# Norm factor as a diagonal matrix in the turn of token tiles, all tiles loaded at once, two weight tiles on the first 512 tokens

## The chip, the core and the metric

One core of a Trainium2 chip. The time is device microseconds of one execution, the median of three runs. The engines are TensorE (PE, with its weight loads as PEld), VectorE (DVE), ScalarE (ACT), GpSimd (POOL) and SyncE (SP), which issues most DMAs.

## What is computed

One layer of a hybrid encoder block on 1024 tokens of 1024 features, in float32. The change touches only its first step and its first projection:

```python
hn = x * rsqrt(mean(x * x, -1) + EPS) * attn_norm     # RMSNorm
proj = hn @ w_in                                      # 1024 x 2728 columns
# proj feeds three head groups: gated delta rule, pooling, latent attention
x = x + concat(groups) @ w_out
x = x + (silu(gate) * up) @ w_down                    # SwiGLU on RMSNorm(x)
```

## The kernel before

The code is written by hand for five engines, each with its own program, which meet at counted semaphores: `wait_ge(sem, n)` holds an engine's whole program until the count is reached, and everything behind it waits too.

**Turn.** The projection needs tokens along the free axis, so the eight tiles of 128 tokens (TT = 8) are normalised and turned. Per tile t: ACT squares x and sums along the row (L1048, `x_sumsq`), running three tiles ahead; POOL makes the factor (L874, L875, `x_rstd`); VectorE scales x by it (L1320, `x_scale`, into `x_scaled`, `raw_used`); TensorE transposes the eight 128x128 blocks into a pair of PSUM banks (L1808, `x_turned`); VectorE multiplies by the gain of `attn_norm` into `stage` (L1329, `x_gain`, `bank_pair_free`); ACT rounds to the high part `act_hi` (L1061, `stage_read`); VectorE subtracts for the low part `act_lo` (L1336, `x_low`, `h_ready`). VectorE's order is scale t+1, low t-1, gain t.

**Projection.** Every product is three passes of f32r: high x high, high x low, low x high. `gemm` (L1812 to L1833) takes 8 k-blocks, 3 passes and 2 halves of 512 tokens: 48 matmuls per weight tile (L1829). Tile m = 0 is a narrow one of 40 columns (`small_raw`: the gates and the rotary key), split in two: its first half may start at `h_ready` = 4, the second at 8; both also need its `w_lo` (L1347). Tiles m = 1 to 21 have 128 columns. ACT makes `w_hi` and VectorE `w_lo` of tile m + 2 when `gemm_done` reaches m + 1 (two slots). After tile 1 stand small transposes (L1846) of what tile 0 gave.

**Loads.** Four buffers `raw` hold first x tiles, then w_in tiles. SP issues in order: x 0 to 3, small_raw, six constants, x 4 to 7 (each waiting until the scale of tile t - 4 has freed its buffer, L525), six more small loads, then w_in tiles (L554, waiting on `raw_used`), with 2 MB of zeros written after m = 2 (L605). ACT issues eight loads of small rows, which VectorE and TensorE turn into `cols` (L1801, L1802, L1314) before the first tile.

## Time and profile before

| | us |
|---|---|
| Runs before, median of 3 | 1370.69 |
| Lowest, highest | 1370.59, 1374.19 |
| The profiled execution's own time | 1367.57 |
| Its span | 1365.7 |
| TensorE busy in the span | 1278.0 (94%) |
| VectorE, ACT, POOL busy | 803.4, 458.5, 392.0 |
| Mean granted clock of TensorE | 0.969 of full |

The profile is of one execution. Times of rows are from the start of its span. The chain of waits is followed back from the last instruction, so what stands on it sets the end. A duration of a matmul is its latency; the distance from start to start is what one costs in a row of them. The granted clock is 1.00 at 2.4 GHz and 0.50 at 1.2 GHz.

### The profile page before, as it was taken

The page shows a single profiled execution, that of the slowest core. Times are in us where ns is not written, and L with a number is a line of the kernel's source. Part 1 is how long each engine was busy: PE and PEld are TensorE (multiplying, and loading weights), DVE is VectorE, ACT ScalarE, POOL GpSimd, SP SyncE. Part 2 cuts the span into 40 slices and gives each one's busy share as a digit, 9 for nine tenths or more (in the row PEclk, how much of TensorE's full clock was granted, in tenths as well). Part 3 has the DMA queues.
Part 4 walks back from the last instruction along what each step waited for, and adds up shares of the span by engine and source line. Part 5 has one row for each costly group of instructions (what it writes and reads, how often), then busy time and mean ns, then how long its engine had stood idle before and what let it go on. Part 6 is the DMA issues. An engine that isn't in the chain of part 4 may idle for free.

```text
span 1365.7 us, 17092 instructions
## 1 busy us (share of the span) xinstructions
PE 1278.0 (94%) x6028; PEld 1011.6 (74%) x6028; DVE 803.4 (59%) x1290; ACT 458.5 (34%) x758; POOL 392.0 (29%) x359
## 2 busy tenths in 40 slices
PE   4899999999788888899978899999999998999998
PEld 3588777887577777744446788888888886888886
DVE  5436788466265655522345466665565559686776
ACT  4231332441332333312234233333333344243442
POOL 3001011330122121200163575565646526200000
PEclk7899999999899999999989999999999999999999
DMA  6411243535722211012131566564456338665634
GB/s 195 127 48 31 74 121 106 151 132 131 239 75 60 75 46 58 0 65 104 47 93 47 169 218 213 187 209 160 154 188 251 127 98 291 204 212 153 212 114 164
DMA packets 188980, 182.62 MB, mean 134 GB/s; under 512 B 19486, under 2 KB 145772, under 8 KB 188908
## 3 DMA queue, kind: packets, MB, share of 16 engines
q1 hardware_dynamic: 188784, 181.64, 42.3%
q8 instruction: 43, 0.70, 0.2%
q14 instruction: 29, 0.24, 0.1%
q10 hardware_dynamic: 124, 0.04, 0.0%
HBM read 123.97 MB, written 56.62 MB: 132 GB/s over the span
## 4 chain that ended last, share of the span: by engine, by line
PE 77%; DVE 11%; issue 5%; ACT 3%; POOL 2%; DMA 1%; SPq 0%; ACTq 0%; DVEq 0%; POOLq 0%; PEldq 0%
PE ps L2161 30%; PE ps L2166 13%; PE ps L1829 12%; PE ps L2077 8%; PE ps L1953 5%; PE ps L2026 3%; PE ps L2054 2%; PE ps L2042 1%; DVE stage L1475 1%; DVE row_stat L1678 1%; POOL mla_sc L895 1%; DVE dop_lo L1734 1%; DVE x L1791 1%; PE ps L1958 1%; PE ps L1974 1%
## 5 line engine op out<-in xcount | busy, mean ns | idle before, releaser
L2161 PE MATMUL ps<-xop_hi,wop_hi 128*128 128x512 f32 x616 | 242.5, 394 | 17.6 <-DVE wop_lo L1728 10.2
L2161 PE MATMUL ps<-xop_hi,wop_lo 128*128 128x512 f32 x616 | 242.0, 393 | 0.0
L2161 PE MATMUL ps<-xop_lo,wop_hi 128*128 128x512 f32 x616 | 241.9, 393 | 0.0
L2161 PEld LDWEIGHTS ps<-xop_hi,wop_hi 128*128 128x128 f32 x616 | 117.0, 190 | 44.1 <-DVE wop_lo L1728 11.2
L2161 PEld LDWEIGHTS ps<-xop_hi,wop_lo 128*128 128x128 f32 x616 | 116.9, 190 | 24.5
L2161 PEld LDWEIGHTS ps<-xop_lo,wop_hi 128*128 128x128 f32 x616 | 116.9, 190 | 24.3
L2166 PE MATMUL ps<-dop_hi,wop_hi 128*128 128x512 f32 x308 | 121.2, 394 | 7.3 <-DVE x L1791 7.3
L1728 DVE TENSOR_TENSOR wop_lo<-w_sumS,wop_hi 128x512 fp32r<-128x512 f32 (+1 forms) x104 | 85.4, 823 | 70.4 <-ACT wop_hi L1250 70.4
L2166 PE MATMUL ps<-dop_hi,wop_lo 128*128 128x512 f32 x308 | 120.6, 392 | 0.0
L2166 PE MATMUL ps<-dop_lo,wop_hi 128*128 128x512 f32 x308 | 120.6, 392 | 0.0
L1829 PE MATMUL ps<-act_hi,w_hi 128*128 128x512 f32 (+1 forms) x352 | 116.4, 408 | 3.8 <-DVE w_lo L1347 3.6
L1728 DVE TENSOR_TENSOR wop_lo<-w_pair,wop_hi 128x512 fp32r<-128x512 f32 (+1 forms) x78 | 88.1, 1132 | 46.8 <-ACT wop_hi L1250 46.8
L2077 PE MATMUL ps<-w_out_sb,oT 128*128 128x512 f32 x256 | 111.4, 592 | 0.0
L1829 PE MATMUL ps<-act_lo,w_hi 128*128 128x512 f32 (+1 forms) x352 | 111.1, 393 | 0.0
L1829 PE MATMUL ps<-act_hi,w_lo 128*128 128x512 f32 (+1 forms) x352 | 111.0, 393 | 0.0
L1791 DVE TENSOR_TENSOR x<-x,ps 128x512 f32<-128x512 f32 x112 | 76.6, 684 | 42.2 <-PE ps L2166 42.1
L2077 PEld LDWEIGHTS ps<-w_out_sb,oT 128*128 128x128 f32 x256 | 47.9, 190 | 56.9 <-issue 56.9
L1354 DVE TENSOR_TENSOR w_lo<-raw,w_hi 128x1024 fp32r<-128x1024 f32 x21 | 26.2, 1250 | 98.1 <-ACT w_hi L1066 98.1
L1250 ACT ACTIVATE wop_hi<-w_sumS 128x512 fp32r<-128x512 f32 (+1 forms) x104 | 63.2, 609 | 60.5 <-PE ps L2161 37.0
L1829 PEld LDWEIGHTS ps<-act_hi,w_hi 128*128 128x128 f32 (+1 forms) x352 | 64.8, 187 | 22.6 <-issue 5.5
L1829 PEld LDWEIGHTS ps<-act_lo,w_hi 128*128 128x128 f32 (+1 forms) x352 | 65.6, 186 | 15.6 <-issue 0.7
L1829 PEld LDWEIGHTS ps<-act_hi,w_lo 128*128 128x128 f32 (+1 forms) x352 | 65.4, 186 | 15.8 <-issue 1.0
(281 smaller groups left out, 2156.2 us busy)
## 6 DMA issues: line engine op xcount, KB each, us to landing
w_pair<-in_w_gate_up SPq DMA_DIRECT2D x44, 512.0 KB, 5.4
hidden<-up SPq DMA_DIRECT2D x22, 512.0 KB, 3.0
wd_rows<-in_w_down SPq DMA_DIRECT2D x22, 512.0 KB, 4.9
raw<-in_w_in SPq DMA_DIRECT2D x21, 512.0 KB, 4.3
wd_raw<-down_sums SPq DMA_DIRECT2D x12, 768.0 KB, 8.5
...
```

Of the source, the lines that this page charges most:

```text
L895: pool.tensor_tensor(mla_sc[t % 2][:, 24:32], mla_sc[t % 2][:, 16:24], half_neg[:, 0:8], ALU.pow).then_inc(mla_pow, 1)
L1250: act.activation(wop_hi[q % RING][:, 0:kh, :], src, ACT.Copy).then_inc(wop_high, 1)
L1354: dve.tensor_tensor(w_lo[slot][:, :, :], raw[rawslot][:, :, :], w_hi[slot][:, :, :].bitcast(f32), ALU.subtract).then_inc(raw_used, 1)
L1728: dve.tensor_tensor(wop_lo[q % RING][:, 0:kh, :], src, wop_hi[q % RING][:, 0:kh, :].bitcast(f32), ALU.subtract).then_inc(wop_ready, 1)
L1791: dve.tensor_tensor(part, part, bank, ALU.add).then_inc(added, 1)
L1829: last = pe.matmul(ps[0:rows, pair + h, :], w[:, k, 0:rows], a[:, k, h * BANK:(h + 1) * BANK], start=(k == 0 and w is whi and a is a_hi), ...
L1953: last = pe.matmul(ps[:, out_bank, h * P:(h + 1) * P], lhs(h), rhs(h), start=True, stop=True)
L2026: last = pe.matmul(ps[:, 4 + h, 0:n], qh[0:QK, t * P:(t + 1) * P], kT[0:QK, ds(i, 1), h * BANK:h * BANK + n].rearrange("p a n -> p (a n)") ...
L2054: last = pe.matmul(ps[:, 7, 0:V_DIM], probsT[0][:, j, :], V[:, kt, ds(i, 1), :].rearrange("p a d -> p (a d)"), start=(kt == 0), stop=(kt = ...
L2077: last = pe.matmul(ps[:, op_pair[t] + h, :], oT[:, t, k, :], w_out_sb[:, k, h * BANK:(h + 1) * BANK], start=(k == 0), stop=(k == KT - 1))
L2161: last = pe.matmul(ps[:, bank, :], w[:, k, :], a[:, k, :], start=(p in ("P1", "P2", "P7") and k == 0 and w is wop_hi[s] and a is hi), stop ...
L2166: last = pe.matmul(ps[:, bank, :], w[:, k, :], a[:, k, :], start=(p in ("P1", "P2", "P7") and k == 0 and w is wop_hi[s] and a is hi), stop ...
```

## The change

- VectorE no longer scales. POOL multiplies the identity by the factors of the tile's tokens (`x_diag`, two of them), and TensorE multiplies each block of raw x with that matrix moving, so that one product turns and scales it.
- Tiles 4 to 7 go to places of their own (the three `cT` rows and one `pz` row, used later by others), so all eight loads wait for no buffer; the second four wait once for the small rows. The constants are issued after weight tile 2, the zeros after weight tile 6.
- Turning uses PSUM banks 4 to 7, so banks 0 to 3 can hold weight tiles 0 and 1 for both halves. Their first halves over tokens 0 to 511 run around the last turn (`early_gemm`), their second halves after `h_ready` = 8. The splits of `small_raw` and of weight tile 1 move into the turn.
- VectorE's order becomes gain t, low t-1; `x_gain(t)` still waits for `h_ready` of t - 1.
- `raw_used` no longer counts the eight scales, so `N_X` goes; counts that used it are renumbered.

```diff
--- before.py
+++ after.py
@@ -254,7 +254,8 @@
     kr_sq = sgT[:, 3, 576:832].rearrange("p (t n) -> p t n", t=TT)
     assert KT * SMALL <= 320
     x_sq = prep[:, 0, :]
-    x_scaled = [prep[:, 1 + s, :] for s in range(2)]
+    x_diag = [prep[:, 1 + s, 0:P] for s in range(2)]
+    x_in = [raw[t][:, :, :].rearrange("p k n -> p (k n)") for t in range(RAW)] + [cT[:, j, :] for j in range(3)] + [pz[:, 0, :]]
     C_CONV, C_ATTN, C_FFN, C_QA, C_KVA, C_GDN, C_POOL, C_POS, C_QK = 0, 48, 56, 64, 66, 67, 68, 70, 78
     ctx = ExitStack()
...
@@ -508,9 +509,11 @@
         def raw_round(gi, j):
             return (j // 3 if gi == 0 else (3, 0, 2, 2)[raw_slot(gi, j)] + ((gi - 1) * 7 + j) // 4) + 1
-        def loaded_count(n):
-            return 16 * (n // RAW + 1) - (16 if n % RAW == 0 else 0)
+        def loaded_count(m):
+            return 16 * (1 + m // RAW + (1 if m % RAW else 0))
+        def x_here(t):
+            return (x_loaded[t], 16) if t < RAW else (x_late[t - RAW], 16)
         w_in_v = w_in[0].rearrange("(k p) n -> p k n", p=P)
@@ -519,39 +522,37 @@
         @block.sync
         def _(sp):
-            def load_x(t):
-                if t >= RAW:
-                    sp.wait_ge(raw_used, t - RAW + 1)
-                sp.dma_start(raw[t % RAW][:, :, :].rearrange("p k n -> p (k n)"),
-                             x[0, t * P:(t + 1) * P, :]).then_inc(x_loaded[t % RAW], 16)
             for t in range(RAW):
-                load_x(t)
+                sp.dma_start(x_in[t], x[0, t * P:(t + 1) * P, :]).then_inc(x_here(t)[0], 16)
             sp.dma_start(small_raw[:, :, 0:2 * GDN_HEADS], w_in_v[:, :, OFF_A:OFF_POOL]).then_inc(small_loaded, 16)
             sp.dma_start(small_raw[:, :, 2 * GDN_HEADS:SMALL],
                          w_in_v[:, :, OFF_KR:OFF_KR + ROPE]).then_inc(small_loaded, 16)
-            sp.dma_start(ab_rows[:, 0, :], a_log[0].partition_broadcast(P)).then_inc(prep_loaded, 16)
-            sp.dma_start(ab_rows[:, 1, :], dt_bias[0].partition_broadcast(P)).then_inc(prep_loaded, 16)
-            sp.dma_start(wuq[:, :, :], w_uq[0].rearrange("(k p) n -> p k n", p=P)).then_inc(prep_loaded, 16)
-            sp.dma_start(wukv[:, :], w_ukv[0]).then_inc(prep_loaded, 16)
-            sp.dma_start(qk_gain[:, 0, :], q_norm[0].partition_broadcast(P)).then_inc(prep_loaded, 16)
-            sp.dma_start(qk_gain[:, 1, :], k_norm[0].partition_broadcast(P)).then_inc(prep_loaded, 16)
+            sp.wait_ge(rows_loaded, 8 * 16)
             for t in range(RAW, TT):
-                load_x(t)
-            sp.wait_ge(consts_ready, 1)
-            for g in range(POOL_GROUPS):
-                lo = (g % 2) * POOL_DIM
-                sp.dma_start(pw[lo:lo + POOL_DIM, g // 2, lo:lo + POOL_DIM], pool_w[0, g]).then_inc(pw_loaded, 16)
-            for j, gain in enumerate((q_norm, k_norm)):
-                sp.dma_start(cols[0:NOPE, C_QK + j:C_QK + j + 1],
-                             gain[0, 0:NOPE].rearrange("(p o) -> p o", o=1)).then_inc(pw_loaded, 16)
+                sp.dma_start(x_in[t], x[0, t * P:(t + 1) * P, :]).then_inc(x_here(t)[0], 16)
+            def load_constants():
+                sp.dma_start(ab_rows[:, 0, :], a_log[0].partition_broadcast(P)).then_inc(prep_loaded, 16)
+                sp.dma_start(ab_rows[:, 1, :], dt_bias[0].partition_broadcast(P)).then_inc(prep_loaded, 16)
+                sp.dma_start(wuq[:, :, :], w_uq[0].rearrange("(k p) n -> p k n", p=P)).then_inc(prep_loaded, 16)
+                sp.dma_start(wukv[:, :], w_ukv[0]).then_inc(prep_loaded, 16)
+                sp.dma_start(qk_gain[:, 0, :], q_norm[0].partition_broadcast(P)).then_inc(prep_loaded, 16)
+                sp.dma_start(qk_gain[:, 1, :], k_norm[0].partition_broadcast(P)).then_inc(prep_loaded, 16)
+                sp.wait_ge(consts_ready, 1)
+                for g in range(POOL_GROUPS):
+                    lo = (g % 2) * POOL_DIM
+                    sp.dma_start(pw[lo:lo + POOL_DIM, g // 2, lo:lo + POOL_DIM], pool_w[0, g]).then_inc(pw_loaded, 16)
+                for j, gain in enumerate((q_norm, k_norm)):
+                    sp.dma_start(cols[0:NOPE, C_QK + j:C_QK + j + 1],
+                                 gain[0, 0:NOPE].rearrange("(p o) -> p o", o=1)).then_inc(pw_loaded, 16)
             def load_in_tile(m, s):
-                sp.wait_ge(raw_used, N_X + m - RAW + 1)
+                if m <= RAW:
+                    sp.wait_ge(x_turned, m % RAW + 1)
+                else:
+                    sp.wait_ge(raw_used, m - RAW + 1)
                 sp.dma_start(raw[s][:, :, :], w_in_v[:, :, ds(proj_col(m), P)]).then_inc(x_loaded[s], 16)
             def keep_qkv(f):
@@ -588,7 +589,9 @@
             KEEP_LAG = 7
             for m in range(1, IN_ALL + KEEP_LAG):
                 if m < IN_ALL:
-                    load_in_tile(m, (N_X + m) % RAW)
+                    load_in_tile(m, m % RAW)
+                if m == 2:
+                    load_constants()
                 done = m - KEEP_LAG
                 if M_QKV <= done < M_GATE:
                     keep_qkv(done - M_QKV)
...
@@ -872,8 +875,11 @@
             for t in range(TT):
                 pool.wait_ge(x_sumsq, t + 1)
                 link(pool.tensor_scalar(meansq[:, t:t + 1], ssq[:, t:t + 1], 1.0 / D_MODEL, EPS, ALU.mult, ALU.add))
-                pool.tensor_tensor(rstd[:, t:t + 1], meansq[:, t:t + 1], half_neg[:, 0:1],
-                                   ALU.pow).then_inc(x_rstd, 1)
+                link(pool.tensor_tensor(rstd[:, t:t + 1], meansq[:, t:t + 1], half_neg[:, 0:1], ALU.pow))
+                if t >= 2:
+                    pool.wait_ge(x_turned, t - 1)
+                pool.tensor_tensor(x_diag[t % 2], ident[:, :], rstd[:, t:t + 1].broadcast_to([P, P]),
+                                   ALU.mult).then_inc(diag_ready, 1)
             pool.memset(zeros[:, :, :], 0.0).then_inc(zeros_ready, 1)
...
@@ -1042,10 +1048,10 @@
             def x_square(t):
-                act.wait_ge(x_loaded[t % RAW], 16 * (t // RAW + 1))
+                act.wait_ge(*x_here(t))
                 if t >= 1:
                     act.wait_ge(x_sumsq, t)
-                act.activation(x_sq, raw[t % RAW][:, :, :].rearrange("p k n -> p (k n)"), ACT.Square,
+                act.activation(x_sq, x_in[t], ACT.Square,
                                accum_out=ssq[:, t:t + 1]).then_inc(x_sumsq, 1)
             AHEAD = 3
@@ -1054,9 +1060,12 @@
             for t in range(TT):
                 if t + AHEAD < TT:
                     x_square(t + AHEAD)
-                if t == TT - 2:
+                if t == 2:
                     act.wait_ge(small_loaded, 2 * 16)
                     act.activation(w_hi[0][:, :, 0:SMALL], small_raw, ACT.Copy).then_inc(hi_split, 1)
+                if t == 5:
+                    act.wait_ge(x_loaded[1], loaded_count(1))
+                    act.activation(w_hi[1][:, :, :], raw[1][:, :, :], ACT.Copy).then_inc(hi_split, 1)
                 act.wait_ge(bank_pair_free, t + 1)
                 act.activation(act_hi[:, :, tile_cols(t)], stage[t % 2][:, :].rearrange("p (k n) -> p k n", k=KT),
                                ACT.Copy).then_inc(stage_read, 1)
@@ -1065,17 +1074,12 @@
                 act.wait_ge(x_loaded[rawslot], rnd)
                 act.activation(w_hi[slot][:, :, :], raw[rawslot][:, :, :], ACT.Copy).then_inc(hi_split, 1)
-            def in_round(m):
-                return loaded_count(N_X + m)
-            split_hi(1, 1, 1, in_round(1))
             act.wait_ge(sin_args, 1)
             act.activation(trig[:, :, :, :].rearrange("p a t f -> p (a t f)"), sin_in, ACT.Sin).then_inc(trig_ready, 1)
             for m in range(M_QKV):
                 act.wait_ge(gemm_done, m + 1)
-                split_hi(m + 2, m % 2, (N_X + m + 2) % RAW, in_round(m + 2))
+                split_hi(m + 2, m % 2, (m + 2) % RAW, loaded_count(m + 2))
                 if M_CQ <= m < M_POOL:
                     act.wait_ge(bank_pair_free, TT + m + 1)
                     act.activation(c_sq[:, m - 1, :], cT[:, m - 1, :], ACT.Square).then_inc(lat_squared, 1)
...
@@ -1311,21 +1315,14 @@
             dve.wait_ge(rows_loaded, 8 * 16)
             dve.tensor_copy(pos_f, pos_i[0:TT, :]).then_inc(pos_float, 1)
             dve.wait_ge(cols_in_psum, 1)
-            link(dve.tensor_copy(cols[:, 0:C_POS + TT], ps[:, 7, 0:C_POS + TT]))
-            def x_scale(t):
-                dve.wait_ge(x_rstd, t + 1)
-                if t >= 2:
-                    dve.wait_ge(x_turned, t - 1)
-                dve.tensor_scalar(x_scaled[t % 2], raw[t % RAW][:, :, :].rearrange("p k n -> p (k n)"),
-                                  rstd[:, t:t + 1], None, ALU.mult).then_inc(raw_used, 1)
+            link(dve.tensor_copy(cols[:, 0:C_POS + TT], ps[:, 3, 0:C_POS + TT]))
             def x_gain(t):
                 dve.wait_ge(x_turned, t + 1)
                 if t >= 2:
                     dve.wait_ge(h_ready, t - 1)
-                pair = (t % 2) * 2
+                pair = 4 + (t % 2) * 2
                 dve.tensor_tensor(stage[t % 2][:, :].rearrange("p (k n) -> p k n", k=KT),
                                   ps[:, pair:pair + 2, :].rearrange("p a (k n) -> p (a k) n", n=P),
                                   cols[:, C_ATTN:C_ATTN + KT].unsqueeze(2).broadcast_to([P, KT, P]),
@@ -1336,17 +1333,18 @@
                 dve.tensor_tensor(act_lo[:, :, tile_cols(t)], stage[t % 2][:, :].rearrange("p (k n) -> p k n", k=KT),
                                   act_hi[:, :, tile_cols(t)].bitcast(f32), ALU.subtract).then_inc(h_ready, 1)
-            x_scale(0)
             for t in range(TT):
-                if t + 1 < TT:
-                    x_scale(t + 1)
+                x_gain(t)
                 if t >= 1:
                     x_low(t - 1)
-                if t == TT - 1:
+                if t == 3:
                     dve.wait_ge(hi_split, 1)
                     dve.tensor_tensor(w_lo[0][:, :, 0:SMALL], small_raw, w_hi[0][:, :, 0:SMALL].bitcast(f32),
                                       ALU.subtract).then_inc(raw_used, 1)
-                x_gain(t)
+                if t == 6:
+                    dve.wait_ge(hi_split, 2)
+                    dve.tensor_tensor(w_lo[1][:, :, :], raw[1][:, :, :], w_hi[1][:, :, :].bitcast(f32),
+                                      ALU.subtract).then_inc(raw_used, 1)
             x_low(TT - 1)
             def split_lo(m, slot, rawslot):
@@ -1389,8 +1387,6 @@
             def pair_of(m):
                 return ps[:, (m % 2) * 2:(m % 2) * 2 + 2, :].rearrange("p a n -> p (a n)")
-            split_lo(1, 1, 1)
             ang_v = ang.rearrange("p (t f) -> p t f", t=TT)
             link(dve.tensor_tensor(ang_v, cols[:, C_POS:C_POS + TT].unsqueeze(2).broadcast_to([P, TT, HALF]),
                                    inv_freq.unsqueeze(1).broadcast_to([P, TT, HALF]), ALU.mult))
...
@@ -1798,26 +1794,35 @@
             pe.wait_ge(consts_ready, 1)
             pe.wait_ge(pos_float, 1)
-            pe.transpose(ps[:, 7, 0:C_POS], rows, ident[0:C_POS, 0:C_POS])
-            pe.transpose(ps[:, 7, C_POS:C_POS + TT], pos_f, ident[0:TT, 0:TT]).then_inc(cols_in_psum, 1)
-            for t in range(TT):
-                pe.wait_ge(raw_used, t + 1)
+            pe.transpose(ps[:, 3, 0:C_POS], rows, ident[0:C_POS, 0:C_POS])
+            pe.transpose(ps[:, 3, C_POS:C_POS + TT], pos_f, ident[0:TT, 0:TT]).then_inc(cols_in_psum, 1)
+            def turn_x(t):
+                pe.wait_ge(diag_ready, t + 1)
                 if t >= 2:
                     pe.wait_ge(bank_pair_free, t - 1)
                 for k in range(KT):
-                    last = pe.transpose(ps[:, (t % 2) * 2 + k // 4, (k % 4) * P:(k % 4 + 1) * P],
-                                        x_scaled[t % 2][:, k * P:(k + 1) * P], ident[:, :])
+                    last = pe.matmul(ps[:, 4 + (t % 2) * 2 + k // 4, (k % 4) * P:(k % 4 + 1) * P],
+                                     x_in[t][:, k * P:(k + 1) * P], x_diag[t % 2], start=True, stop=True)
                 last.then_inc(x_turned, 1)
-            def gemm(whi, wlo, a_hi, a_lo, pair, kts, signal, rows=P, tail=None, late_half=None, middle=None):
-                passes = [(0,), (1,)] if late_half else [(0, 1)]
-                for halves in passes:
-                    if halves == (1,):
-                        pe.wait_ge(*late_half)
+            def early_gemm(m, h, ks):
+                rows = SMALL if m == 0 else P
+                for k in ks:
+                    for w, a in ((w_hi[m], act_hi), (w_hi[m], act_lo), (w_lo[m], act_hi)):
+                        last = pe.matmul(ps[0:rows, 2 * m + h, :], w[:, k, 0:rows], a[:, k, h * BANK:(h + 1) * BANK],
+                                         start=(k == 0 and w is w_hi[m] and a is act_hi), stop=(k == KT - 1 and w is w_lo[m]),
+                                         skip_group_check=True)
+                return last
+            for t in range(TT - 1):
+                turn_x(t)
+            def gemm(whi, wlo, a_hi, a_lo, pair, kts, signal, rows=P, tail=None, middle=None):
+                for halves in [(0, 1)]:
                     for k in range(kts):
                         if tail and k == kts - 1:
                             pe.wait_ge(*tail)
@@ -1834,12 +1839,20 @@
             pe.wait_ge(h_ready, TT // 2)
-            pe.wait_ge(raw_used, N_X + 1)
-            gemm(w_hi[0], w_lo[0], act_hi, act_lo, 0, KT, gemm_done, SMALL, late_half=(h_ready, TT))
+            pe.wait_ge(raw_used, 1)
+            early_gemm(0, 0, range(0, KT // 2))
+            turn_x(TT - 1)
+            early_gemm(0, 0, range(KT // 2, KT))
+            pe.wait_ge(raw_used, 2)
+            early_gemm(1, 0, range(KT))
+            pe.wait_ge(h_ready, TT)
+            early_gemm(0, 1, range(KT)).then_inc(gemm_done, 1)
+            early_gemm(1, 1, range(KT)).then_inc(gemm_done, 1)
             for m in range(1, M_QKV):
-                pe.wait_ge(raw_used, N_X + m + 1)
-                pe.wait_ge(bank_pair_free, TT + m - 1)
-                gemm(w_hi[m % 2], w_lo[m % 2], act_hi, act_lo, (m % 2) * 2, KT, gemm_done)
+                if m >= 2:
+                    pe.wait_ge(raw_used, m + 1)
+                    pe.wait_ge(bank_pair_free, TT + m - 1)
+                    gemm(w_hi[m % 2], w_lo[m % 2], act_hi, act_lo, (m % 2) * 2, KT, gemm_done)
                 if m == 1:
                     pe.wait_ge(bank_pair_free, TT + 1)
                     for t in range(TT):
...
```

## Rows read from the trace of the kernel before

**Rows 1.** The chain of waits, 0 to 70 us: start us, us, what.

```profile
24.09 1.23 DVE stage L1329
38.66 24.18 PE ps L1829 x96
```

**Rows 2.** Timeline of one period: start, us, engine, line, op [idle before <-releaser].

```profile
25.23 0.75 DVE L1320 TENSOR_SCALAR prep<-raw,rstd 128x1024 f32<-128x1024 f32 x1
26.03 1.97 PE L1808 MATMUL ps<-ident,prep 128*128 128x128 f32 x8 [1.52 <-DVE prep L1320]
26.44 1.22 DVE L1336 TENSOR_TENSOR act_lo<-stage,act_hi 128x1024 fp32r<-128x1024 f32 x1 [0.46 <-ACT act_hi L1061]
27.58 1.22 DVE L1329 TENSOR_TENSOR stage<-ps,cols 128x1024 f32<-128x1024 f32 x1
```

**Rows 3.** TensorE's waits, 0 to 130 us: total us, times, longest.

```profile
PE ps L1808 <- DVE prep L1320: 11.0, 7, 3.0
```

**Rows 4.** Windows: us, then PE, PEld, DVE, ACT, POOL busy, PEclk, DMA, GB/s.

```profile
22.50:24.60 2.10, 1.97 (x8) 1.56 (x8) 1.65 (x2) 1.46 (x3) 0.47 (x2) 0.50 0.04 1
42.00:42.90 0.90, 0.90 (x3) 0.37 (x2) 0.90 (x1) 0.90 (x1) 0.00 (x0) 0.50 0.31 75
42.90:44.00 1.10, 1.10 (x6) 0.61 (x5) 1.00 (x5) 0.09 (x1) 0.00 (x0) 0.95 0.08 19
```

**Rows 5.** The timeline, the first turns and GpSimd's first step.

```profile
6.33 0.19 POOL L874 TENSOR_SCALAR meansq<-ssq 128x1 f32<-128x1 f32 x1 [2.18 <-ACT prep L1048]
9.50 0.27 PE L1802 MATMUL ps<-ident,prep 8*128 8x8 f32 x1
10.89 3.67 PE L1808 MATMUL ps<-ident,prep 128*128 128x128 f32 x16 [1.12 <-DVE prep L1320]
18.32 1.26 PE L1808 MATMUL ps<-ident,prep 128*128 128x128 f32 x8 [2.00 <-DVE prep L1320]
```

**Rows 6.** The timeline, two chained operations on VectorE.

```profile
45.66 0.30 DVE L1409 TENSOR_SCALAR prep<-prep 128x256 f32<-128x256 f32 x1
45.99 0.42 DVE L1410 TENSOR_TENSOR prep<-prep 128x256 f32<-128x256 f32 x1
```

**Rows 7.** Single operations: the timeline, then a group by form.

```profile
24.32 0.55 POOL L875 TENSOR_TENSOR rstd<-meansq,half_neg 128x1 f32<-128x1 f32 x1
25.35 1.06 ACT L1061 ACTIVATE act_hi<-stage 128x1024 fp32r<-128x1024 f32 x1 [1.39 <-DVE stage L1329]
26.31 1.04 ACT L1048 ACTIVATE prep<-raw 128x1024 f32<-128x1024 f32 x1
27.26 0.19 ACT L1048 ACTIVATION_READ_ACCUMULATOR prep<-raw 128x1 f32 x1
38.03 0.49 DVE L1347 TENSOR_TENSOR w_lo<-sgT,w_hi 128x320 fp32r<-128x320 f32 x1
...
L904 POOL TENSOR_TENSOR gtg<-gt,g_log 128x512 f32<-128x512 f32 x8 | 8.2, 1044 | 0.0
```

**Rows 8.** Transfers: chain (last small row), line L526 (x tiles), timeline (tile 4).

```profile
3.44 5.36 DMA pos_i<-in_positions
...
DMA to landing us min/median/max: 4.1/5.4/7.1
...
17.34 1.06 ACT L1048 ACTIVATE prep<-raw 128x1024 f32<-128x1024 f32 x1 [2.12 <-DMA raw<-in_x]
```

**Rows 9.** The timeline: clock up, weight tile 1 begins, what follows it.

```profile
42.92 0.44 PE L1829 MATMUL ps<-act_lo,w_hi 128*40 128x512 f32 x1
51.78 0.62 PE L1829 MATMUL ps<-act_hi,w_hi 128*128 128x512 f32 x2
62.76 0.58 PEld L1846 LDWEIGHTS ps<-ident,prep 40*128 40x128 f32 x8 [0.35 <-issue]
```

**Rows 10.** The chain, whole span: f32 128x128 multiplies L1953, transposes L2069.

```profile
365.52 1.84 PE ps L1953 x16
573.04 1.94 PE ps L2069 x16
```

16 lines of the change are left out of this document (8 added, 8 removed).

## Prediction, made before the changed kernel was run

> **What bounds the kernel now.** I read the page first (TensorE is busy 94% of the span), then the chain of waits over the first 70 us, the timeline of that stretch, and the granted clock by windows. The chain shows two pieces there. Up to 38.66 us it alternates between the stages of turning a token tile; from 38.66 us on it is TensorE's own projection, 96 matmuls without a wait [rows 1]. So everything that starts or shortens those 96 matmuls (weight tiles 0 and 1) moves the end, and after them nothing is tied to the clock on the wall: later stages count on `gemm_done` and `raw_used`.
>
> In the turn VectorE sets the pace. One period, from one gain multiply to the next, is 27.58 - 24.09 = 3.49 us [rows 1, 2]: scale L1320 0.75, low part L1336 1.22, gain L1329 1.22, and gaps in which VectorE waits for what it had asked of others. TensorE waits 11.0 us in seven places for the scaled tile [rows 3], and needs 1.97 us of each period for its eight transposes, since its clock is at half there [rows 2, 4].
>
> **Part by part.** Removed: eight scales on VectorE (0.75 each). Added: on GpSimd one 128x128 multiply per tile; TensorE multiplies raw x by the diagonal in place of transposing scaled x. Moved: x tiles 4 to 7 no longer wait for a buffer; six constants and the 2 MB of zeros go behind them on SP; the halves of tiles 0 and 1 over the first 512 tokens go ahead of the last turn.
>
> *Start.* Turn 0 stood behind the first scale, at 10.89 us; now the diagonal hangs on the sum of squares, which GpSimd takes up at 6.33 us [rows 5]; its three operations there, some 0.2 + 0.6 + 0.4 with gaps, end by 7.8 us. So turn 0 follows the transposes of the rows directly: 9.50 + 0.27, about 9.84 us. Sixteen took 3.67 us [rows 5], so turn 1 ends at 13.5 and the gain of tile 1 starts at 13.6.
>
> *VectorE's new period.* Gain, low, gain, low. A following independent instruction starts 1.14 us after the last (26.44 to 27.58) [rows 2], but the gain of t+1 now waits for the low part just before it, so it is 1.22 and the wait on its own completion, 0.03 us by the chained pair at 45.66 [rows 6]: 1.26. A period is 2.41. Gains start at 13.6, 16.0, 18.4; then low 2, the small w_lo (0.49 [rows 7]), and gain 4 at 21.15, ending 22.4. Low 3 ends at 23.5: four tiles ready.
>
> *What else could set that pace.* ACT needs 1.04 + 0.19 for a square and 1.06 for a high part [rows 7], 2.3 against 2.41: it just fits, and the small w_hi (a third of a tile, so under 0.5) goes into its lead. GpSimd needs 0.19 [rows 5], 0.55 and the new multiply. The trace has no 128x128 one; bounds are a quarter of L904's 1.04, 0.26, and the whole of it [rows 7]. I take 0.4. The diagonal of tile 6 is then ready at about 21.8, against 22.4 when its bank is free; at 1.04 it is 22.4, so the cost is nil, and 0.3 beyond. TensorE at half clock needs 1.97 per tile, under 2.41.
>
> *Loads.* SP waits for the rows, landed at 3.44 + 5.36 = 8.80, then issues x 4 to 7. An x tile lands 4.1 to 7.1 us after issue [rows 8], so x 4 is there between 13.0 and 16.0; ACT wants it at 14.2. In the worst case high part 1 ends at 18.3 where VectorE wants it at 17.15: 0 to 1.15 us, and I take 0, the first of a group of four landing early. In the kernel before, ACT got tile 4 only at 17.34 [rows 8], but there the transfer could not be issued before the first scale had freed its buffer, at about 10.9. The constants on SP stand in front of weight tile 3 alone, which nobody needs before the end of tile 1 (about 50 us): over 30 us of cover from their start near 16 us. The eight issues of zeros, moved to m = 6, are in front of weight tile 7, used some 40 us later. Both at nothing; without the cover each would cost what it is late.
>
> *TensorE from there.* Turn 6 runs 22.4 to 24.4, then the early halves. Until the clock rises a matmul takes (42.92 - 38.66)/10 = 0.426, after it (51.78 - 42.92)/38 = 0.233 for tile 0; tile 1's 48 take 62.76 - 51.78 = 10.98 [rows 1, 9]. In the rows the granted clock is 0.50 (the level of 1.2 GHz) until the projection has run some 4.3 us, then full (2.4 GHz) [rows 4]. So: 10 x 0.426 = 4.26, 38 x 0.233 = 8.86, 10.98, and one warm turn 1.26 [rows 5] in their midst: 25.36, ending at 49.8 us instead of 62.76. **Saving 13.0 us.** All 48 first-half matmuls end near 38.5; the eighth low part, behind the last turn, ends near 34, so the second halves don't wait (4 us of slack). The small w_lo and tile 1's, at 21.1 and 29.7, are early as well.
>
> *The multiply in place of the transpose.* Sixteen real f32 128x128 multiplies take 1.84 us and sixteen f32 transposes 1.94 [rows 10]: no difference. I take a ratio of 1. The Trainium skill says the contrary: Perfetto Trace Analysis, Transposes, asks that a logical transpose use the transpose and not a standard matmul, and TensorE: Matmul & The Clock Gate, Terms, calls the transpose mode four times faster for FP32. By that rule the turn would take four times as long, and the time would be that of the second rival at its far end; the trace disagrees [rows 10].
>
> The sum against the profiled execution: span 1365.7 - 13.0 = 1352.7, its time 1367.57 - 13.0 = 1354.6. That execution lies 3.1 us under the median of the runs, 1370.69; from the median, **1357.7 us**.
>
> **Rivals.**
> 1. *The clock is up early.* Turns are closer together (1.97 of 2.41 us busy instead of 1.97 of 3.49), and turn 6 leads straight into the projection. If it is full from turn 6 on: turn 6 is 0.71 shorter, ten matmuls 0.193 each: 2.6 us more, 1355.1. Against: a turn of 1.26 us at full speed at 18.32 [rows 5] did not hold it up; by 22.5 us it was at 0.50 [rows 4]. Between lies the case that the 4.3 us count from turn 6: 0.9 more.
> 2. *The multiply costs f transposes (slower at f = 4).* Nothing shows the exact pair of operands, so f from 1 to 4 stays possible. Place: turns 0 to 6 on TensorE. At f = 4 it would be bound there: 9.84 + 4.3 cold (0.55 of a tile), 6.45 x 5.04 warm, then 22.0 for 96 warm matmuls and 5.04 for turn 7: 73.7, 10.9 us later than now, 1381.6. With a ratio f the end is 33.4 + 10.1 f; it decides from f = 2.9. At f = 2 it is 53.6, a saving of 9.2, 1361.5. Against both stand [rows 10].
> 3. *ACT or the x tiles set the pace.* A square of a late tile stands ahead of the high part of an earlier one on ACT. With x 4 at 16.0 the sum loses 1.15; with a further 0.2 for each of five periods, as ACT has just 0.1 to spare, some 2 to 3 us: 1360.2. For it: ACT's 2.3 is close; against it: the squares run three tiles ahead, so one late step is caught up.
> 4. *The saving is not seen.* The early halves are in place but a later wait absorbs them: 1370.7. I found none, as every load has its cover.
>
> **How the numbers follow.** My forecast, 1356 to 1359, has 0.58; rival 1 0.15; rival 2 at f = 2 0.06, at f = 4 0.04; rival 3 0.12; rival 4 0.05. 0.3% of the time, 4.1 us, is about what a measurement can tell from no change. The first case with its own bounds is 1355.5 to 1360 (clock 0.9 more, x 4 late 1.15 less, and 1 us of scatter). The range reaches from rival 1 with 1.6 us of scatter, 1353.5, over rival 3 and f = 2 to 1364, and leaves f = 4 and rival 4 out. Faster: 0.58 + 0.15 + 0.06 + 0.12 = 0.91; same 0.05; slower 0.04.
>
> **What would show it.** In the profile after: turn 0 near 9.8 us; gains 2.4 us apart; eight products of a turn in about 2 us cold; the first w_hi matmul at 24 to 25 us; tile 1 done near 50; the small transposes right behind; no wait of TensorE for `act_lo` in the second halves. Wrong: a turn of 4 us or more (rival 2), ACT ending VectorE's waits in every period or idle for DMA x (rival 3), the projection at 0.23 us from its first matmul (rival 1), or a new wait of the matmuls of weight tile 3 or 7 for a load.

## The result, and the profile after

The changed kernel takes 1358.71 us (median; 1354.88 to 1361.91), the kernel before 1370.87 beside it. The ratio is 0.9907, with an interval of 0.9889 to 0.9925: about 12 us, or 0.9%, faster. The forecast was 1357.7. Run again with the last experiments it took 1357.62 against 1372.30, ratio 0.989 (0.9875 to 0.9904).

The profiled execution took 1358.45 us with a span of 1356.7, against 1365.7 before. From the head of the page, the busy times:

```profile
PE 1285.6 (95%) x6092; PEld 1022.4 (75%) x6092; DVE 794.9 (59%) x1282; ACT 459.0 (34%) x758; POOL 399.3 (29%) x367
```

TensorE executes 6092 instructions; the page of before has 6028. The forecast counted on none more, and here are 64. Next the chain of waits over 0 to 70 us, which answers to [rows 1]:

```profile
9.91 6.20 PE ps L1804 x32
...
16.13 1.23 DVE stage L1326
17.36 1.14 DVE act_lo L1333
...
18.59 1.23 DVE stage L1326
...
25.09 2.02 PE ps L1804 x16
27.11 2.79 PE ps L1812 x12
29.90 1.78 PE ps L1804 x16
31.68 19.29 PE ps L1812 x84
50.98 0.63 PE ps L1859 x8
```

The projection (L1812) begins at 27 instead of 38.66 us, and the small transposes (L1859) follow tile 1 at 51 instead of 62.76. The first line is new: two turns with 32 instructions stand at the head of the chain. The timeline of TensorE and of VectorE shows the same stretch:

```profile
9.84 9.83 PE L1804 MATMUL ps<-prep,raw 128*128 128x128 f32 x64
19.96 2.02 PE L1804 MATMUL ps<-prep,cT 128*128 128x128 f32 x16 [0.30 <-DVE stage L1326]
26.87 0.48 PE L1812 MATMUL ps<-act_hi,w_hi 128*40 128x512 f32 x1
27.18 0.39 PE L1812 MATMUL ps<-act_lo,w_hi 128*40 128x512 f32 x1
27.41 0.40 PE L1812 MATMUL ps<-act_hi,w_lo 128*40 128x512 f32 x1
...
29.74 1.95 PE L1804 MATMUL ps<-prep,pz 128*128 128x128 f32 x16
```

```profile
13.74 1.23 DVE L1326 TENSOR_TENSOR stage<-ps,cols 128x1024 f32<-128x1024 f32 x1 [3.55 <-PE ps L1804]
16.13 1.23 DVE L1326 TENSOR_TENSOR stage<-ps,cols 128x1024 f32<-128x1024 f32 x1 [1.17 <-PE ps L1804]
17.27 1.22 DVE L1333 TENSOR_TENSOR act_lo<-stage,act_hi 128x1024 fp32r<-128x1024 f32 x1
18.59 1.23 DVE L1326 TENSOR_TENSOR stage<-ps,cols 128x1024 f32<-128x1024 f32 x1
```

A turn has eight products in the code and 16 instructions in the trace. The first takes 3.90 us (9.84 to the gain at 13.74), a later one 2.02. I call TensorE cold where it runs at half its later rate, as here: 10 instructions fall into the window from 10 to 12 us, 11 into the next and 20 into that from 16 to 18 us. The column of the granted clock reads 1.00 in all of them, so for the first turns it doesn't show this. The same kernel in another execution (e11) ended its second turn 0.3 us later than this one, counted from the start of its first. Gains then come 18.59 - 16.13 = 2.46 us apart instead of 3.49, and the first matmuls of the projection already stand 0.23 us apart. For the matmuls the granted clock says why. By windows of ten microseconds (PE, PEld, DVE, ACT, POOL busy; granted clock; DMA), first the kernel before, then the changed one:

```profile
20.00:30.00 10.00, 4.36 (x18) 3.56 (x19) 8.67 (x10) 5.72 (x9) 3.72 (x10) 0.50 0.34 99
30.00:40.00 10.00, 4.85 (x20) 3.35 (x19) 8.17 (x8) 2.79 (x4) 2.20 (x5) 0.50 0.98 306
```

```profile
20.00:30.00 10.00, 8.91 (x63) 7.25 (x64) 9.69 (x10) 7.15 (x10) 8.70 (x17) 1.00 0.81 217
30.00:40.00 10.00, 10.00 (x53) 7.53 (x52) 9.55 (x19) 3.36 (x3) 0.00 (x0) 1.00 0.26 65
```

Before, TensorE was busy 4.4 of 10 us while turning and its clock was at 0.50 (1.2 GHz); now it is busy 8.9 of 10 us and the clock stays at 1.00 (2.4 GHz) in both windows. The busy share alone doesn't decide it: from 20 to 30 us the kernel e4 below is busy 5.6 us at 1.00, and e3 6.5 us at 0.50, where each instruction takes longer.

The stretch from the first transpose of the rows to the small transposes behind tile 1 I call the front. It took 53.55 us before (9.22 to 62.77) and takes 41.55 now (9.36 to 50.91): 12.0 us. The medians differ by 12.2 us, and by 14.7 in the second set of runs. Two single executions compare less well further on: at the transposes L2069 of [rows 10], L2082 after, the distance is 573.04 - 565.34 = 7.7 us. From the small transposes to those the profile before needed 510.3 us and this one 514.4. All kernels below scatter there between 509 and 517 us, nearly all of it unchanged code, with no clear relation to the front. The length does go with the granted clock from 300 to 570 us: the profiles with 0.94 there took 509.4 to 512.1 us, those with 0.93 took 512.5 to 513.2, those with 0.92 took 514.4 to 516.8. The kernel before, then the changed one:

```profile
300.00:570.00 270.00, 236.72 (x1547) 200.41 (x1546) 151.80 (x386) 82.97 (x160) 48.38 (x43) 0.94 0.30 88
```

```profile
300.00:570.00 270.00, 235.47 (x1531) 200.31 (x1531) 148.60 (x389) 80.94 (x162) 44.48 (x38) 0.92 0.29 84
```

So I compare fronts by one profile each, and times by the medians. The medians resolve no more than two or three microseconds: less the front, the kernels still differ by some 6 us.

### The profile page after: what moved, and what is told of

It is laid out like the page before. It is cut to its first block, busy times and chain, and to the rows that moved or that the text cites. A ratio compares the mean times of both kernels' runs of the same rounds, so it can differ in the third digit from the quotient of the medians.

```text
span 1356.7 us, 17219 instructions
## 1 busy us (share of the span) xinstructions
PE 1285.6 (95%) x6092; PEld 1022.4 (75%) x6092; DVE 794.9 (59%) x1282; ACT 459.0 (34%) x758; POOL 399.3 (29%) x367
## 4 chain that ended last, share of the span: by engine, by line
PE 79%; DVE 10%; issue 4%; ACT 3%; POOL 2%; DMA 1%; ACTq 0%; DVEq 0%; SPq 0%; POOLq 0%; PEldq 0%
PE ps L2174 30%; PE ps L2179 14%; PE ps L1834 10%; PE ps L2090 8%; PE ps L1966 5%; PE ps L2039 3%; PE ps L2067 2%; PE ps L1812 2%; PE ps L2055 1%; DVE stage L1471 1%; DVE row_stat L1674 1%; POOL mla_sc L901 1%; PE ps L1804 1%; PE ps L1971 1%; PE ps L1987 1%
## 5 line engine op out<-in xcount | busy, mean ns | idle before, releaser
L1834 PE MATMUL ps<-act_hi,w_hi 128*128 128x512 f32 x320 | 104.3, 407 | 0.2 <-DVE stage L1471 0.2
L1834 PE MATMUL ps<-act_lo,w_hi 128*128 128x512 f32 x320 | 99.6, 393 | 0.0
L1834 PE MATMUL ps<-act_hi,w_lo 128*128 128x512 f32 x320 | 99.3, 392 | 0.0
L1254 ACT ACTIVATE wop_hi<-w_pair 128x512 fp32r<-128x512 f32 (+1 forms) x78 | 47.6, 612 | 82.2 <-issue 54.6
L2179 PEld LDWEIGHTS ps<-dop_hi,wop_hi 128*128 128x128 f32 x308 | 58.3, 189 | 20.5 <-DVE wop_lo L1724 5.8
L1834 PEld LDWEIGHTS ps<-act_hi,w_hi 128*128 128x128 f32 x320 | 59.9, 190 | 15.8 <-issue 4.7
```

Of the source, the lines that this page charges most:

```text
L1254: act.activation(wop_hi[q % RING][:, 0:kh, :], src, ACT.Copy).then_inc(wop_high, 1)
L1834: last = pe.matmul(ps[0:rows, pair + h, :], w[:, k, 0:rows], a[:, k, h * BANK:(h + 1) * BANK], start=(k == 0 and w is whi and a is a_hi), ...
L2179: last = pe.matmul(ps[:, bank, :], w[:, k, :], a[:, k, :], start=(p in ("P1", "P2", "P7") and k == 0 and w is wop_hi[s] and a is hi), stop ...
```

## The experiments

Fronts and times of all, in microseconds; each ratio is against the kernel before, on the same chip:

| kernel | front | median | ratio (interval) |
|---|---|---|---|
| before | 53.55 | 1370.87 | 1 |
| changed | 41.55 | 1358.71 | 0.9907 (0.9889 to 0.9925) |
| plain transposes, factor left out (e1) | 38.71 | 1356.88 | 0.989 (0.9876 to 0.9904) |
| the same, each transpose issued twice (e2) | 40.17 | 1356.86 | 0.9895 (0.988 to 0.9909) |
| scale on VectorE (e3) | 43.88 | 1361.07 | 0.9923 (0.9911 to 0.9935) |
| low part before the next gain (e4) | 45.50 | 1363.86 | 0.9946 (0.9933 to 0.9959) |
| no early halves (e5) | 42.80 | 1362.33 | 0.9924 (0.9898 to 0.995) |
| small `w_lo` late (e6) | 47.55 | 1360.97 | 0.9917 (0.9901 to 0.9934) |
| x tiles through four buffers (e7) | 41.74 | 1357.00 | 0.9899 (0.9879 to 0.9919) |
| first two tiles scaled (e8) | 39.29 | 1353.38 | 0.9862 (0.9845 to 0.9879) |
| changed, again (e11) | 41.86 | 1357.62 | 0.989 (0.9875 to 0.9904) |
| e8, again (e12) | 38.98 | 1354.76 | 0.9866 (0.985 to 0.9883) |
| e12 with a third stage (e13) | 38.22 | 1355.39 | 0.988 (0.9866 to 0.9895) |
| before, two moves alone (e14) | 47.95 | 1362.70 | 0.9925 (0.9909 to 0.9941) |

For e8, e12 and e13 the front is counted from turn 0, which now comes first (at 8.60, 8.29 and 8.05 us).

### Is it the product or the number of instructions?

```diff
-                    last = pe.matmul(ps[:, 4 + (t % 2) * 2 + k // 4, (k % 4) * P:(k % 4 + 1) * P],
-                                     x_in[t][:, k * P:(k + 1) * P], x_diag[t % 2], start=True, stop=True)
+                    last = pe.transpose(ps[:, 4 + (t % 2) * 2 + k // 4, (k % 4) * P:(k % 4 + 1) * P],
+                                        x_in[t][:, k * P:(k + 1) * P], ident[:, :])
```

> The changed kernel, but TensorE turns the raw tile with a real transpose (moving operand the identity, still waiting for the diagonal); the norm factor is left out of the result. My theory: the product of two f32 operands is two TensorE instructions for each block (128 in all), a transpose is one (64). So here turns 0 and 1 end near 13.5 us instead of 16.1, the gains start 2.5 us sooner and the projection begins at 24.4 instead of 26.9; but with 1.97 or 1.3 of each 2.45 us busy the clock is not held up, and ten matmuls run at half, so that tile 1 ends near 49.8 instead of 51.0: about 1357.5 us. Rival (one instruction each, the 2.5 us come from elsewhere): start of the projection unchanged at 26.9, 1358.7 us. If the clock stays full all the same: tile 1 ends near 47.2, 1355.

The second kernel issues each of these transposes twice, in a loop around the call (excerpt):

```diff
+                    for again in range(2):
```

Both leave the norm factor out of what they compute.

> As the plain turn, but every transpose is issued twice into the same place; norm factor left out. My theory (the price is the second instruction, and its busy time keeps the clock full): 128 instructions, turn 0 ends at 13.7, projection begins at 26.9 at 0.233 us per matmul from the first, tile 1 ends at 51.0, 1358.7 us. Rival (a true multiply is slower for another reason than the number of instructions): shorter turns than the changed kernel's 2.02 us at full clock.

The timeline of TensorE in e1, then in e2:

```profile
10.03 6.60 PE L1804 MATMUL ps<-ident,raw 128*128 128x128 f32 x32
17.57 1.07 PE L1804 MATMUL ps<-ident,cT 128*128 128x128 f32 x8 [0.94 <-DVE stage L1326]
22.70 1.86 PE L1804 MATMUL ps<-ident,cT 128*128 128x128 f32 x8 [1.60 <-DVE stage L1326]
```

```profile
9.73 8.51 PE L1805 MATMUL ps<-ident,raw 128*128 128x128 f32 x64
18.62 1.94 PE L1805 MATMUL ps<-ident,cT 128*128 128x128 f32 x16 [0.38 <-DVE stage L1326]
```

A transpose is one instruction and a product of two float32 operands is two. Sixteen issued transposes take 1.94 us and the 16 instructions of eight products 2.02: the matrix itself costs nothing more than its second instruction. That holds for the turns at full rate. The front is 41.55 - 38.71 = 2.84 us shorter with eight instructions than in the changed kernel, but only 1.46 us shorter than in e2, and the difference lies ahead of gain 1 (the gain multiply of tile 1). From gain 1 to the small transposes the three need nearly the same: 34.78 us in the changed kernel, 34.63 in e2, 34.52 in e1. So the second instruction costs 1.5 to 2.8 us of front, nearly all of it in the two cold turns.

In the clock the two part. In e1 the windows 22 to 24 and 24 to 26 us show 0.70 and 0.50, and turn 6 takes 1.86 us for what turn 4 did in 1.07; in e2, as in the changed kernel, the clock stays at 1.00. The slow stretch in e1 held only turn 6 and some four or five matmuls, where I had expected ten, so tile 1 ended 1.5 us earlier than expected. In e2 the two cold turns were quicker than in the changed kernel (9.73 to gain 1 at 14.79, 5.1 us, against 9.84 to 16.13, 6.3), and tile 1 ended 1.6 us earlier than expected: 18 instructions already fall into its window from 12 to 14 us, 11 in the changed kernel. Why TensorE came to its full rate sooner there isn't shown; the kernels below that turn tiles 0 and 1 with the same products need 5.9 to 6.6 us for this stretch, so part of it may be scatter. e1 starts the projection 1.2 us sooner than e2 (24.21 against 25.45) and loses 0.9 us to the slow matmuls. The medians of the two are alike, so 1.46 us of front are not seen in the time.

### Which part of the change carries the gain?

Four kernels undo one part each. The scale goes back to VectorE and TensorE transposes the scaled tile again, without GpSimd's diagonal; everything else stays (excerpt):

```diff
+            def x_scale(t):
+                dve.wait_ge(x_rstd, t + 1)
+                if t >= 2:
+                    dve.wait_ge(x_turned, t - 1)
+                dve.tensor_scalar(x_scaled[t % 2], x_in[t], rstd[:, t:t + 1], None, ALU.mult).then_inc(diag_ready, 1)
```

> The changed kernel with the diagonal undone: VectorE scales each tile again and TensorE transposes it, while VectorE's new order (gain t before low t-1), the loads and the early halves stay. My theory: the old period of 3.49 us was a loop over two engines, gain, high part on ACT, low part, gain, not the sum of VectorE's work; with the new order the scale adds just its 0.67, period 3.1 us, projection from 27.7 us, ten matmuls at half clock, tile 1 ends near 53: 1360.8 us. Rival (the scale was what set the old period): period back at 3.49, projection from about 30.5, 1364 us.

The period was 2.93 us (gains at 15.30, 18.23 and 21.16), the projection came at 29.21, 1.5 us later than expected, and the clock fell to 0.50 from about 19 us on, with eight-instruction turns again. The front is 2.33 us longer than the changed one: this is the diagonal's part, net of its second instructions. In the time it is 1361.07 us, with an interval that overlaps the changed kernel's.

VectorE's order goes back, low part of t - 1 ahead of gain t:

```diff
             for t in range(TT):
-                x_gain(t)
                 if t >= 1:
                     x_low(t - 1)
+                x_gain(t)
```

> The changed kernel with one thing undone: VectorE takes low t-1 before gain t again. My theory: the loop gain 1.23, high part 1.06, low part 1.14 with waits is back, period 3.5 us although no scale is left; fourth low part ends near 28.1, turn 6 at 31.4, projection from 31.4 at half clock at first, tile 1 ends near 57: 1364.5 us. Rival (the period is the sum of VectorE's work, 2.4): unchanged, 1358.7 us.

The chain of waits in e4:

```profile
17.37 1.15 DVE stage L1326
18.52 0.02 issue
18.54 1.06 ACT act_hi L1070
19.61 0.02 issue
19.63 0.03 DVE act_lo L1333
19.66 1.11 issue
20.77 1.23 DVE stage L1326
```

Gains come 20.77 - 17.29 = 3.48 us apart, the very period of before (3.49), although VectorE has no scale at all. The chain runs from gain to high part on ACT to low part to the next gain, 1.15 + 1.06 + 1.14 us and small gaps. So what bound the turns before was this loop, made by the order, and not VectorE's sum: the 0.75 us scale filled a wait inside the loop. The clock stayed at 1.00 in e4 with 16-instruction turns even at this period, where I had expected it to fall.

No halves ahead of the last turn:

```diff
-            for t in range(TT - 1):
+            for t in range(TT):
                 turn_x(t)
...
-            early_gemm(0, 0, range(0, KT // 2))
-            turn_x(TT - 1)
-            early_gemm(0, 0, range(KT // 2, KT))
+            early_gemm(0, 0, range(KT))
...
```

The second half of tile 0 also moves ahead of tile 1.

> The changed kernel without the early halves: all eight turns first, then tile 0 in halves and tile 1 whole after eight tiles are ready, as in the kernel before. My theory: TensorE has 4 to 5 us of waits to fill here at most, since the eighth low part (35.6 us) is out soon after the first half of tile 0 ends (35.0); tile 1 ends near 52.1 instead of 51.0, so the early halves are worth about 1 us: 1359.8 us. Rival (the early halves carry the saving, by overlapping half of two tiles with the turn): the projection's 48 first-half matmuls, 11 us, are added again, 1368 us.

The front grew by 1.25 us, as expected. The median, 1362.33 and not 1359.8, is higher than this explains: its profile has 516.4 us in the later stretch, the upper end of the scatter.

The small tile's `w_lo` moves from behind low 2 to behind low 5:

```diff
-                if t == 3:
+                if t == 6:
                     dve.wait_ge(hi_split, 1)
                     dve.tensor_tensor(w_lo[0][:, :, 0:SMALL], small_raw, w_hi[0][:, :, 0:SMALL].bitcast(f32),
                                      ALU.subtract).then_inc(raw_used, 1)
-                if t == 6:
                     dve.wait_ge(hi_split, 2)
```

> The changed kernel with the low part of the small weight tile (0.49 us of VectorE) taken after low part 5 instead of low part 2. Theory: the first half of tile 0 waits for it, from 26.9 to about 31.1 us, and with TensorE idle so long the clock may drop: tile 1 ends near 55 us (full clock) or 57 (half at first), 1362.8 to 1364.7 us. Rival (the place of so small an operation does not matter, the fourth token tile does): 51.0, 1358.7.

Timeline of TensorE, and windows, in e6:

```profile
30.58 0.40 PE L1811 MATMUL ps<-act_hi,w_hi 128*40 128x512 f32 x1 [4.52 <-DVE w_lo L1342]
30.81 0.40 PE L1811 MATMUL ps<-act_lo,w_hi 128*40 128x512 f32 x1
...
31.83 0.63 PE L1811 MATMUL ps<-act_lo,w_hi 128*40 128x512 f32 x1
```

```profile
30.00:32.00 2.00, 1.42 (x5) 0.74 (x6) 1.56 (x2) 0.00 (x0) 0.09 (x1) 0.78 0.01 2
32.00:34.00 2.00, 2.00 (x7) 0.78 (x6) 0.00 (x0) 0.00 (x0) 0.00 (x0) 0.50 0.63 163
34.00:36.00 2.00, 2.00 (x14) 1.60 (x13) 0.00 (x0) 0.00 (x0) 0.00 (x0) 0.87 0.33 99
```

TensorE stands idle 4.5 us for one small operation of some 0.5 us. The clock then falls to 0.50 for about 3 us, after the matmuls have begun, which makes up the rest of the 6.0 us. By the front this is the largest single part. The time doesn't bear that out: 1360.97 us, below the 1362.8 to 1364.7 expected, and a ratio whose interval overlaps the changed kernel's. Of the four only the old order of VectorE (e4) is clear of the changed kernel in time. In the kernel before the same operation stood at the last tile, and held the projection the same way; its timeline around 38 us:

```profile
38.03 0.49 DVE L1347 TENSOR_TENSOR w_lo<-sgT,w_hi 128x320 fp32r<-128x320 f32 x1
38.66 0.62 PE L1829 MATMUL ps<-act_hi,w_hi 128*40 128x512 f32 x1 [3.59 <-DVE w_lo L1347]
```

### Do the loads matter?

Tiles 4 to 7 go through the four `raw` buffers again, each waiting for the turn of tile t - 4 (the counts of loads are renumbered for it, and the first weight tiles wait behind them):

```diff
-    x_in = [raw[t][:, :, :].rearrange("p k n -> p (k n)") for t in range(RAW)] + [cT[:, j, :] for j in range(3)] + [pz[:, 0, :]]
+    x_in = [raw[t % RAW][:, :, :].rearrange("p k n -> p (k n)") for t in range(TT)]
...
-            sp.wait_ge(rows_loaded, 8 * 16)
             for t in range(RAW, TT):
+                sp.wait_ge(x_turned, t - RAW + 1)
                 sp.dma_start(x_in[t], x[0, t * P:(t + 1) * P, :]).then_inc(x_here(t)[0], 16)
```

> The changed kernel, with x tiles 4 to 7 loaded through the four buffers again, each once its buffer has been turned, and the first weight tiles behind them. Theory: x 4 is issued at 13.8 and lands 4.1 to 6.4 us later; on ACT its square stands ahead of high part 1, so low parts 1 and 2 slip by up to 3 us, then ACT's 2.3 us per tile holds the pace: tile 1 ends 2 to 3.5 us later than 51.0, 1361 to 1362 us. Rival (loads are hidden at this pace too): 1358.7.

ACT's timeline in e7:

```profile
16.52 1.06 ACT L1054 ACTIVATE prep<-raw 128x1024 f32<-128x1024 f32 x1 [1.15 <-DMA raw<-in_x]
...
17.58 1.04 ACT L1070 ACTIVATE act_hi<-stage 128x1024 fp32r<-128x1024 f32 x1
19.21 1.06 ACT L1054 ACTIVATE prep<-raw 128x1024 f32<-128x1024 f32 x1 [0.59 <-DMA raw<-in_x]
```

I had expected a front 2 to 3.5 us longer and got 0.19. ACT does wait for the late tiles, by 1.15 and 0.59 us, but it works ahead and caught up by tile 6. Places of their own for tiles 4 to 7 are worth 0.2 us of front here, or 0.5 if counted from gain 1 (35.32 us against 34.78), and the time of the kernel can't tell that from nothing. This kernel keeps the other half of the change to the loads, the constants behind the x tiles. Its tile 4 was issued at 12.97 us and ACT had it at 16.52; in e14 below, with the constants just ahead on SP's queue, it was issued at 11.46 and ACT had it at 17.87. No run moves the constants alone.

### Two moves alone in the kernel before

Gain t goes ahead of low t - 1, and the small `w_lo` to tile 3, with its high part at tile 2 and a semaphore `small_low` of its own. `raw_used` still counts it at the last tile, and TensorE waits besides for the gain of tile 6 to free its banks. Nothing else is changed (excerpt):

```diff
+                x_gain(t)
                 if t >= 1:
                     x_low(t - 1)
-                if t == TT - 1:
+                if t == 3:
...
-            pe.wait_ge(raw_used, N_X + 1)
+            pe.wait_ge(small_low, 1)
```

> The kernel before with two small moves alone, no diagonal, no early halves, loads as they were: VectorE takes gain t ahead of low t-1, and the small weight tile's low part is taken after low part 2 instead of before gain 7. Theory: the loop over ACT is broken, the projection begins after the eighth turn, near 32.7 us instead of 38.7, at half clock; about 6 of the 12 us in the front, 1366 us. Rival (without the diagonal VectorE's own work holds the period, and the loads of x 4 to 7 the rest): less than 2 us, 1370.

The front became 47.95 us: two moves of lines bring 5.6 of the 12.0 us. The median fell by more, 9.6 us or 0.75% (1366 us was expected); the profiled execution is the slowest of its six, so its front may not stand for the others. The rest of the front is out of their reach: VectorE waits once for ACT, held up by tile 4's late square (ACT had waited 3.28 us for the tile),

```profile
20.00 1.23 DVE L1337 TENSOR_TENSOR act_lo<-stage,act_hi 128x1024 fp32r<-128x1024 f32 x1 [1.78 <-ACT act_hi L1062]
```

the scale now lies in the period for real, and the projection starts at 32.83 us at half clock.

### A version that beats both

At the start turn 0 costs 3.90 us of a cold TensorE while VectorE is idle. So tiles 0 and 1 are scaled on VectorE and transposed, turn 0 stands ahead of the transposes of the rows, and only tiles 2 to 7 use the diagonal (excerpt):

```diff
+            for t in range(2):
+                dve.wait_ge(first_rstd, t + 1)
+                dve.tensor_scalar(x_first[t], x_in[t], rstd[:, t:t + 1], None, ALU.mult).then_inc(first_scaled, 1)
```

> A mixed version: tiles 0 and 1 are scaled by VectorE, which has nothing else to do then, and transposed (one instruction per block); the first turn goes ahead of the transposes of the small rows; the other six tiles use the diagonal as in the changed kernel. Theory: the first gain starts at 10.9 us instead of 13.7 and the second at 12.6 instead of 16.1; if x 4 has landed by 13.2, the projection begins at 23.3 instead of 26.9 and runs at full clock, tile 1 ends near 47.4: 1355.2 us. Rival (x 4 lands late, 15 to 16 us, and ACT's square of it holds high part 1): 1 to 2 us less saving, 1356.5.

TensorE's timeline in e8:

```profile
8.60 1.94 PE L1810 MATMUL ps<-ident,stage 128*128 128x128 f32 x8 [8.60 <-DVE stage L1322]
...
10.79 1.97 PE L1810 MATMUL ps<-ident,stage 128*128 128x128 f32 x8
12.55 4.77 PE L1813 MATMUL ps<-prep,raw 128*128 128x128 f32 x32
```

Turns 0 and 1 take 1.94 and 1.97 us, the projection starts at 23.85 at full clock, and the small transposes come at 47.89 instead of 50.91: 3.0 us, with 1353.38 us in the runs. It was run again with the last set, beside the changed kernel and one with a third `stage` buffer, so that the gain of t need not wait for the low part just before it:

> The changed kernel itself again, beside the three below on one chip. Theory: the front is fixed within 0.2 us once the small rows have landed (from the first transpose of the rows to the second small transposes' end, 42.2 us), and the scatter of 7 us among its runs comes from the rounds between 307 and 565 us, where the granted clock falls and rises: 1356 to 1359 us. Rival: the saving in the front is partly given back in the rounds in every run: the rounds' stretch is again 4 us longer than the 509.6 of the kernel before, 1359 us or more.

> The mixed version (tiles 0 and 1 scaled on VectorE) again, beside the changed kernel on one chip. From its first front, 3.0 us shorter than the changed kernel's: 1353 to 1355.5 us.

```diff
-                if t >= 2:
-                    dve.wait_ge(h_ready, t - 1)
+                if t >= 3:
+                    dve.wait_ge(h_ready, t - 2)
```

> The mixed version with a third stage buffer, so that gain t waits for low part t-3 and not for the one just before it. Theory: a gain then starts 1.14 us behind the low part instead of 1.32 (the wait on its own completion), 0.18 for each of five, if ACT's 2.3 us per tile keeps up with a period of 2.28: projection 0.5 to 0.8 us sooner, 1353 us. Rival (that wait costs nothing, or ACT is next): no earlier than 23.8 us, 1353.5.

1354.76 against 1357.62 for the changed kernel fits some 3 us, as the traces do: the small transposes come 3.7 us sooner here, 3.0 in e8, of which 0.8 is an earlier start in both (the fronts differ by 2.9 and 2.3). The two intervals overlap a little, those of e8 and the first runs of the changed kernel don't. The third stage does what it says, gains 16.43 - 14.16 = 2.27 us apart instead of 2.46, and the small transposes come at 46.27 instead of 47.27. Of that 1.0 us, 0.24 is an earlier start of its execution and some 0.36 came ahead of the end of gain 1, where turn 1 took 1.61 instead of 1.97 us; about 0.4 us is left for the third stage. In the time it can't be seen: 1355.39 (1353 was expected) against 1354.76, with overlapping intervals.

## Why the prediction was right, and where only by luck

The time is right within 1 us, and in part by luck: its terms are wrong in opposite directions.

*What bounds the kernel.* Right that everything ahead of the 96 matmuls moves the end. Wrong in "VectorE sets the pace": e4 has the old period without the scale, so the pace was the loop gain, high part, low part, made by VectorE's order. I had the rows for it; in [rows 2] the low part waits for ACT. Nor did I say that the small `w_lo` at the last tile held the start, 3.59 us; the sum had its effect in it, as it took the new start from the new order, but a reader would have put the gain down to the missing scales.

*Start.* Turn 0 forecast at 9.84, measured 9.84. GpSimd's multiply, bounded by 0.26 and 1.04 and taken as 0.4, took 0.40.

*The multiply in place of the transpose.* This is the step that failed. I took a ratio of 1 from [rows 10], 16 of L1953 in 1.84 us against 16 of L2069 in 1.94. But x16 counts instructions. L1953 is the product in `four`, which issues four for each call; its group by operands in that stretch, in the kernel before:

```profile
L1953 PE MATMUL ps<-N,qkvf x8: 275/275/328, 365.4 to 366.2; 128*128 128x128 f32 x8
L1953 PE MATMUL ps<-qkvf,N x8: 275/275/275, 366.3 to 367.1; 128*128 128x128 f32 x8
```

Each call has eight records, so the 16 were eight products, whereas the 16 of L2069 were 16 transposes, as its loops (4 x 2 x 2) say. The ratio was two, rival 2's middle case with 0.06. It cost what its place says: gain 1 at 16.13 instead of 13.6, +2.5, and turn 7 at 1.95 instead of 1.26, +0.7. e1 confirms the place: with transposes gain 1 came at 13.74. Rival 2's own price for this case, tile 1 at 53.6 us and 1361.5, was 2.7 us too high. It doubled a turn of 1.26 us to 2.52, more than VectorE's period, but that turn of [rows 5] was not one at full speed: the granted clock from 18 to 20 us in that profile averages 0.78. At full clock a turn of transposes takes 1.07 us (e1) and one of products 2.02, so TensorE didn't set the pace. The Trainium skill's rule, to use the transpose (Perfetto Trace Analysis, Transposes), was right in direction, by the 1.5 to 2.8 us of e2 and e1; it says nothing of the scale that the product takes along, and the kernel with scale and transposes (e3) had the longer front. The Trainium skill's factor of four (TensorE: Matmul & The Clock Gate, Terms) was not: the trace has two instructions, each of a transpose's length, and 2.02 against 1.07 us a turn.

*VectorE's new period.* 2.41 forecast, 2.46 measured. The term that was mis-sized is the wait on its own completion: the low part of 17.27 ends at 18.49 and the gain starts at 18.59, 0.10 and not the 0.03 of [rows 6]. (The sum itself is a hundredth or two off: 1.22 + 0.03 is 1.25, and the period 2.39.)

*ACT, GpSimd, loads.* ACT just fitted. Tile 4 was there before 15.96, when ACT took it without a wait, as forecast. That a buffer alone kept it back in the kernel before was half the story: in e14 the first scale ends by about 10.2 us and the tile is issued at 11.46, straight behind the last constant. Constants and zeros cost nothing that shows: TensorE waits for no load up to 130 us, and after the first wait for the rows only 1.4 us in all, for banks.

*The clock.* Ten matmuls at 0.426 and turn 6 at half clock did not come: 27.18 to 27.41 us is 0.23 from the first pair on. This was rival 1, worth 2.6 us, of which 1.9 for the ten matmuls. Rival 1 said that denser turns would hold the clock up. They did, but they were dense because of the second instruction I had left out. e1 and e2 show it: with the eight-instruction turns that I had forecast, at the same period, the clock did fall to 0.50, for a shorter time than ten matmuls; with each issued twice it stayed at 1.00.

*Together.* The start of the projection came at 26.87 instead of 24.4 (+2.5), turn 7 cost +0.7, the clock gave back 1.9: tile 1 ended at 50.9 instead of 49.8. Saving 11.9 in place of 13.0. That the clock's term paid back more than half of what the second instructions cost was not foreseen, and is the luck in the number. Rivals 3 and 4 didn't occur. In e7 late tiles cost 0.2 to 0.5 us and not the 2 to 3 us that I gave rival 3, since ACT's lead takes them up; in e14 one that came 3.28 us late did cost VectorE a wait of 1.78 us.

*The parts.* Undone one by one, by the front: the place of the small `w_lo` 6.0 us, VectorE's order 3.95, the diagonal 2.33, the early halves 1.25, the loads 0.19. They add up to 13.7 against 12.0, so they overlap: an undone part leaves cover under which others count less or more. The medians give another order, with e4 5 us above the changed kernel, e5 4, and e3 and e6 2 each; only e4's is clear of it by the intervals.

What stays open: why the stretch after the front varies by several microseconds from kernel to kernel (509 to 517 us). It is longer where its granted clock between 300 and 570 us is lower (0.92 to 0.94 in the profiles); no run separates cause and effect, or says why e6 and e14 differ in time from what their fronts say. Open is also when TensorE leaves its half rate in the first turns.
